# Differential scores: two of the three terms of a map stacked over 128 rows, the third as 64-row pairs

## The reference

```python
def differential_attention(q, k, v, lam):   # q,k: (B,H,2,T,Dh), H = 8, Dh = 64; v: (B,H,T,2Dh)
    def block(args):                         # 128 queries
        s = jnp.einsum('bhiqd,bhikd->bhiqk', qb, k) * scale     # i: the two maps
        s = s - (slopes[:, None, None] * dist[None])[None, :, None]
        p = jax.nn.softmax(s, axis=-1)
        a = p[:, :, 0] - lam * p[:, :, 1]
        return jnp.einsum('bhqk,bhkd->bhqd', a, v)
```

## Time and profile before

| | |
|---|---|
| median of 3 runs (lowest to highest) | 2536.93 us (2536.89 to 2537.68) |
| profiled execution | 2532.99 us, span 2531.0 us |
| mean granted TensorE clock | 0.997 |
| busy: TensorE, VectorE, ScalarE, GpSimd | 2502.5, 1758.6, 1155.8, 413.7 us |
| attention of layer 1 | from 1252 to about 1775 us |

### The profile page before, as it was taken

How to read it: one execution, slowest core, us unless ns; L and a number is a source line. 1 busy time by engine, 2 the same in 40 slices (tenths; PEclk the granted TensorE clock), 3 DMA queues, 4 the chain that set the end, 5 groups by cost and what they waited for, 6 DMA issues and landing times.

```text
span 2531.0 us, 34993 instructions
## 1 busy us (share of the span) xinstructions
PE 2502.5 (99%) x12931; PEld 2065.0 (82%) x12931; DVE 1758.6 (69%) x2647; ACT 1155.8 (46%) x2016; POOL 413.7 (16%) x320
## 2 busy tenths in 40 slices
PE   9999999899999999999999999999999999999998
PEld 7888777688888888888888888888888888888887
DVE  6556565656878878666577777777657878887654
ACT  6555554625333333444455455556343333334434
POOL 1001022400332333100000000000002333232001
PEclk9999999999999999999999999999999999999999
DMA  3222253633444444866211111111334444447764
GB/s 130 61 60 74 53 134 94 186 127 117 147 178 162 146 171 166 316 216 210 80 48 50 50 50 50 48 49 71 117 108 143 168 155 164 156 154 268 237 194 145
DMA packets 189171, 332.38 MB, mean 131 GB/s; under 512 B 59728, under 2 KB 67792, under 8 KB 180816
## 3 DMA queue, kind: packets, MB, share of 16 engines
q1 hardware_dynamic: 154208, 320.62, 37.5%
q10 hardware_dynamic: 34800, 9.60, 1.8%
HBM read 238.24 MB, written 91.91 MB: 130 GB/s over the span
## 4 chain that ended last, share of the span: by engine, by line
PE 93%; issue 2%; DVE 2%; ACT 1%; DMA 1%; SPq 1%; POOL 0%; ACTq 0%; POOLq 0%; DVEq 0%
PE PS L2381 20%; PE PS L2296 18%; PE PS L2297 18%; PE PS L2298 18%; PE PS L2545 4%; PE PS L2477 4%; PE PS L2501 3%; PE PS L2493 1%; PE PS L2448 1%; PE PS L2522 1%; PE PS L2395 1%; PE PS L2462 1%; PE PS L2304 1%; PE PS L2526 1%; PE PS L2438 0%
## 5 line engine op out<-in xcount | busy, mean ns | idle before, releaser
L2381 PE MATMUL PS<-HH,WS 128*128 128x512 f32 x1536 | 515.9, 402 | 3.5 <-DVE HL L1623 1.1
L2381 PEld LDWEIGHTS PS<-HH,WS 128*128 128x128 f32 x1536 | 285.5, 188 | 59.9 <-issue 1.6
L2381 PE MATMUL PS<-HL,WS 128*128 128x512 f32 x768 | 301.4, 393 | 0.0
L2097 DVE TENSOR_TENSOR SPLIT<-RAWI,SPLIT 128x1024 fp32r<-128x1024 f32 x154 | 194.2, 1265 | 149.9 <-ACT SPLIT L1450 149.9
L1450 ACT ACTIVATE SPLIT<-RAWI 128x1024 fp32r<-128x1024 f32 x154 | 162.9, 1060 | 205.7 <-PE PS L2298 152.2
L2296 PE MATMUL PS<-TH,WS 128*128 128x512 f32 x640 | 249.2, 389 | 2.3 <-ACT SIL L1442 2.3
L2298 PE MATMUL PS<-TH,WS 128*128 128x512 f32 x640 | 249.0, 389 | 0.0
L2297 PE MATMUL PS<-TL,WS 128*128 128x512 f32 x640 | 249.0, 389 | 0.0
L2296 PE MATMUL PS<-SPLIT 128*128 128x512 f32 x616 | 240.2, 390 | 0.0
L2298 PE MATMUL PS<-SPLIT 128*128 128x512 f32 x616 | 239.7, 389 | 0.0
L2297 PE MATMUL PS<-SPLIT 128*128 128x512 f32 x616 | 239.7, 389 | 0.0
(11 more groups left out here) (274 smaller groups left out, 4969.8 us busy)
## 6 DMA issues: line engine op xcount, KB each, us to landing
WR<-wstrips SPq DMA_DIRECT2D x224, 256.0 KB, 2.7
RAWI<-ab_scratch SPq DMA_DIRECT2D x154, 256.0 KB, 4.2
ab_scratch<-SIL SPq DMA_DIRECT2D x132, 256.0 KB, 2.0
WD<-wdown SPq DMA_DIRECT2D x22, 1024.0 KB, 7.5
wd_scratch<-WD SPq DMA_DIRECT2D x22, 1024.0 KB, 3.9
RAWI<-wd_scratch SPq DMA_DIRECT2D x88, 256.0 KB, 3.3
UR<-wstrips SPq DMA_DIRECT2D x80, 256.0 KB, 3.3
RAWI<-wdown SPq DMA_DIRECT2D x66, 256.0 KB, 3.8
```

The source lines that it names most:

```text
L2097: e.tensor_tensor(SPLIT[m % 6][:, 1], RAWI[:, m % 4], f(SPLIT[m % 6][:, 0]), ALU.subtract).then_inc(S["ilo"], 1)
L2381: last = e.matmul(ps, wt, xt, start=g == 0, stop=g == 23)
```

## The change

A tile QLOW is added. For layer 1 KS and QS are laid out by map: in slot m the rows of map m hold the high part, and the other 64 rows hold, for K, map m's low part, and for Q, map m's high part again. So one matmul over 128 rows gives high x high + high x low of a map. The third term, Q low x K high, has QLOW and stays in 64-row matmuls, two side by side.

To fill the other rows there is a new ScalarE function `kq_cross`: two copies of 64 x 512 from the staging slot across the halves. `kq_low` writes K's low part back into the staging slot and Q's into QLOW. `kq_high` and `kq_low` are two instructions of 64 rows each instead of one of 128. `kq_cross` for K waits for `kq_low`. It stands behind the exps of the step, and in `begin(1)` between the roundings. `qk` and some evacuations wait for a new semaphore `kq_crossed`; `pick_ready` is folded into `consts_ready`. In `begin(1)` 18 matmuls of chunk 0 go ahead of the first `qk` and 6 behind it.

```diff
@@ pool_program, kq_low(P, k)
+            if P >= 8:
+                for m in range(2):
+                    r = map_rows(m)
+                    high = KS[r, P % 2, m, c:c + 512] if k < 4 else QS[r, m, c:c + 512]
+                    low = staged(k, r) if k < 4 else QLOW[r, c:c + 512]
+                    last = e.tensor_tensor(low, staged(k, r), f(high), ALU.subtract)
+                last.then_inc(S["kq_lo"], 1)
+                return
@@ act_program, kq_high(P, k)
+            if P >= 8:
+                for m in range(2):
+                    r = map_rows(m)
+                    to = KS[r, P % 2, m, c:c + 512] if k < 4 else QS[r, m, c:c + 512]
+                    last = e.activation(to, staged(k, r), ACT.Copy)
+                last.then_inc(S["kq_hi"], 1)
+                return
             e.activation(high[:, c:c + 512], staged(k), ACT.Copy).then_inc(S["kq_hi"], 1)
+
+        def kq_cross(P, k):
+
+            c = 512 * (k % 2)
+            if k < 4:
+                e.wait_ge(S["kq_lo"], 4 * P + k - 1)
+            for m in range(2):
+                to = KS[map_rows(1 - m), P % 2, m, c:c + 512] if k < 4 else QS[map_rows(1 - m), m, c:c + 512]
+                last = e.activation(to, staged(k, map_rows(m)), ACT.Copy)
+            last.then_inc(S["kq_crossed"], 1)
@@ act_program, begin(layer)
-            for k in range(3, 5) if layer else range(2, 6):
-                kq_high(P0, k)
-            if layer == 0:
+            if layer:
+                kq_high(P0, 3)
+                kq_cross(P0, 2)
+                kq_cross(P0, 3)
+                kq_high(P0, 4)
+                kq_cross(P0, 4)
+            else:
+                for k in range(2, 6):
+                    kq_high(P0, k)
@@ act_program, attention_diff()
                     if after:
                         exp(*after, m, "C")
+                for v in rounded(P, n):
+                    kq_cross(*v)
                 if last:
@@ dve_program, evac(P, k, bank=None)
             if late(P):
+                if P >= 8 and k == 2 and P > 8:
+                    e.wait_ge(S["kq_crossed"], crossed_to(P - 1, 5))
+                elif P >= 8 and k in (5, 0, 1):
+                    e.wait_ge(S["kq_crossed"], crossed_to(P, {5: 2, 0: 3, 1: 4}[k]))
@@ pe_program, qk(P, n)
             e.wait_ge(S["kq_lo"], 4 * P + (3 if n < 4 else 4))
+            e.wait_ge(S["kq_crossed"], crossed_to(P, 4 if n < 4 else 5))
             e.wait_ge(S["exp_done"], 1 + 16 * P + 2 * n)
...
-            for c in range(0, nk, 4):
-                wd = 128 * min(4, nk - c)
-                k = slice(128 * (k0 + c), 128 * (k0 + c) + wd)
-                for i, (a, b) in enumerate(((0, 0), (0, 1), (1, 0))):
-                    for m in range(2):
-                        r = slice(64 * m, 64 * m + 64)
-                        last = e.matmul(PS[:, S_BANK[m] + c // 4, 0:wd], QS[r, a, q], KS[r, P % 2, b, k],
-                                        start=i == 0, stop=i == 2)
+            for h in range(2):
+                for m in range(2):
+                    e.matmul(PS[:, S_BANK[m] + h, :], QS[:, m, q], KS[:, P % 2, m, half(h)], start=True, stop=False)
+            for h in range(2):
+                for m in range(2):
+                    r = map_rows(m)
+                    last = e.matmul(PS[:, S_BANK[m] + h, :], QLOW[r, q], KS[r, P % 2, m, half(h)], start=False, stop=True)
@@ pe_program, begin(layer)
-            fill(P0, 0, 0, 14, layer, bank=PV_BANK)
+            fill(P0, 0, 0, 18, layer, bank=PV_BANK)
             qk(P0, 0)
-            fill(P0, 0, 14, 24, layer, bank=PV_BANK)
+            fill(P0, 0, 18, 24, layer, bank=PV_BANK)
```

More of the change, by code:

```diff
@@ L171, in build @@
     PICK = sb("PICK", [128, 64], f32r)
+    QLOW = sb("QLOW", [128, T], f32r)
     assert place[0] <= nc.sbuf_usable_end
@@ L275, in bias_tile, with staged, map_rows, crossed_to @@
         return BIASC[:, par, :] if kind == "C" else (BIAS1 if par else BIAS0)
-    def staged(k):
-        return FS[:, 512 * ((k % 3 + 1) % 3):512 * ((k % 3 + 1) % 3) + 512]
+    def staged(k, r=slice(0, 128)):
+        return FS[r, 512 * ((k % 3 + 1) % 3):512 * ((k % 3 + 1) % 3) + 512]
+    def map_rows(m):
+        return slice(64 * m, 64 * m + 64)
+    def crossed_to(P, k):
+        return 4 * (P - 8) + k - 1
     VFLAT = FS[:, 512:3 * 512 + BAND]
@@ L342, in build @@
                  "hsq_done hhi_done hlo_done hadd hsum_done hsqrt_done hrinv_done hspread_done hrstd_done "
-                 "fill_done fill_evac kq_hi kq_lo tv_done vhi_done vlo_done "
+                 "fill_done fill_evac kq_hi kq_lo kq_crossed tv_done vhi_done vlo_done "
                  "bias_full0 bias_full1 qk_done ttr_done exp_done rec_done "
@@ L347, in build @@
                  "rb_full4 rb_full5 rb_full6 rows_turned rows_copied rows_out rwide_done lspread_done ymul_done st_done st_copy ct_out cn_full cd_done ce_done cw_done al_half al_done a_out mgy_full mgz_full mga_full mg_done ym_out "
-                 "yhi_done ylo_done ysq_done yssq_done yeps_done ymean_done ysqrt_done yrec_done yspread_done ynorm_done rt_turned rt_high rt_low pick_ready op_half "
+                 "yhi_done ylo_done ysq_done yssq_done yeps_done ymean_done ysqrt_done yrec_done yspread_done ynorm_done rt_turned rt_high rt_low op_half "
                  "raw_full2 raw_full3 raw_full4 raw_full5 raw_full6 raw_full7 product_done s_ready copied c11_added c22_added c21_added "
@@ L1966, in attention_diff @@
                     flat = "p k t -> p (k t)"
-                    e.tensor_tensor(PICK[:, :], IDENT[:, 0:64], IDENT[:, 64:128], ALU.add).then_inc(S["pick_ready"], 1)
-                    e.memset(RT[:, KC - 1, :], 1.0).then_inc(S["pick_ready"], 1)
+                    e.tensor_tensor(PICK[:, :], IDENT[:, 0:64], IDENT[:, 64:128], ALU.add).then_inc(S["consts_ready"], 1)
+                    e.memset(RT[:, KC - 1, :], 1.0).then_inc(S["consts_ready"], 1)
                     e.scalar_tensor_tensor(out=EL[:, :, :].rearrange(flat), in0=L0[:, :, :].rearrange(flat),
@@ L2683, in attention_diff @@
             e.wait_ge(S["yrec_done"], 1)
-            e.wait_ge(S["pick_ready"], 2)
+            e.wait_ge(S["consts_ready"], 4 + 2)
             e.transpose(PS[0:64, FILL_BANK, 128:256], RT[:, :, :].rearrange("p k t -> p (k t)"),
```

## The result

| | before | after |
|---|---|---|
| median (lowest to highest) of 4 runs each | 2536.91 us (2536.52 to 2537.68) | 2553.61 us (2552.53 to 2560.76) |
| ratio after / before, 95% interval | | 1.0080 (1.0068 to 1.0092) |
| profiled execution, its span | 2532.99, 2531.0 us | 2553.2, 2551.4 us |
| busy: TensorE, VectorE, ScalarE, GpSimd | 2502.5, 1758.6, 1155.8, 413.7 us | 2507.8, 1761.8, 1218.9, 457.2 us |

The forecast was 2537.7 us (2535.6 to 2542.2) and no change. The kernel is 16.7 us slower, 11.4 us above the range.

The account below looks back on a forecast made before the run. TensorE was taken to bound the kernel, with 93% of the span. Blocks -1.0, start +1.2, pairs +0.2 and tail +0.4 gave +0.8 us: 2537.7 us, range 2535.6 to 2542.2, no change.

Parts of the forecast that it names:

- Together 1.91: Block of scores on TensorE: six slots as before, still 1.91 us; 0.015 us a block won, -1.0 us in all.
- Rival 4: Score blocks: the change of rows behind 128-row matmuls costs nothing, 12.8 us faster, 2525 us; chance 0.06.
- +1.2 us: Start of layer 1: the later first block and longer blocks on an idle array lose 1.2 us of TensorE time.
- I take 1.29: Start of layer 1: GpSimd's two 64-row halves overlap and take 1.29 us together; upper bound 2.55.
- Rival 1: Start of layer 1: GpSimd takes the halves one after the other, +3.2 us in all, 2540.1 us; chance 0.25.
- Two copies in a row take 1.16 us, each further one 0.53: ScalarE: price of 64-row copies, used for the rounding halves and crossings at the start and in the pairs.
- rival 2: Start of layer 1: on top of rival 1 the clock falls, 2541.8 to 2543.5 us, say 2542.5; chance 0.12.
- Theory C: Rival explanation set up for the follow-up runs, not in the forecast: the clock causes the loss; no size given.
- That holds by 0.1 to 0.2 us: Pairs: Q's crossings end in time for the fifth block and the next pair's first, with 0.1 to 0.2 us spare.
- +0.2: The other seven pairs: ScalarE's crossings cost 0.2 us in all, bounds 0 and +4.5.
- Rival 3: Pairs: crossings pass the two gates by 0.2 us at 15 places, +3 us, 2540.7 us; chance 0.12.
- 2 x 0.19 = +0.4: Tail: two blocks of the last pair start behind an exp on an idle array, each 0.19 us longer.

Follow-up runs that it names:

- e1_pairs: Changed kernel with each block of scores again as twelve 64-row matmuls, all roundings, subtractions and crossings as changed; 2554.27 us, ratio 1.0070.
- e4: Kernel before with layer 1's roundings and subtractions split into 64-row halves, no crossings, old matmuls; 2539.41 us, ratio 1.0017.
- e3: Changed kernel with Q's first half rounded ahead of K's crossings at the start of layer 1; 2550.81 us, ratio 1.0060.
- e7: e6 with the crossings at the start of layer 1 on VectorE too; 2539.34 us, ratio 1.0012.
- e8: e7 with the subtraction of Q's first half at the start of layer 1 on VectorE as well; 2538.35 us, ratio 1.0012.
- e2: Changed kernel with crossing copies cut from 512 to 8 columns from P = 10 on; 2544.08 us, ratio 1.0034.
- e10: e6 with the order of e3 at the start of layer 1; 2539.11 us, ratio 1.0008.
- e5: Changed kernel with K's crossings in the pairs moved on ScalarE behind the output copy and weight split; 2553.21 us, ratio 1.0060.
- e9: Pair 8 and the start of layer 1 as in the kernel before, pairs 9 to 15 as e6; 2533.83 us, ratio 0.9992.
- e6: e5 with Q's crossings in the pairs done by VectorE, those at the start of layer 1 still on ScalarE; 2542.07 us, ratio 1.0024.

## Why the prediction was wrong

**The block: right.** "Together 1.91", 0.015 us a block to be won: away from the gates it is 1.897 against 1.905, 0.008 a block, within the bounds. Rival 4 is out, since the 0.32 comes back inside the block. The Trainium skill ("TensorEngine Tiling (Array Packing)", Key Properties) has the array drain where the tiling mode changes, and this agrees. e1_pairs has the same result from the other side. So nothing was there to pay for the feeding.

**The start: "+1.2 us" was +7.0.** Four things made it: the halves on GpSimd, the copies on ScalarE, a term that I left out, and the clock.

**The halves on GpSimd: "I take 1.29".** They took 2.57 to 3.00 us. Rival 1, "GpSimd takes the halves one after the other", at 0.25, was right. The Trainium skill's "GPSIMD Engine Reference", section 2.1, on which I leaned, has each core begin the next instruction when its own share is done; the halves start 1.35 us apart, wherever they stand back to back. So they don't overlap here; why not, no run tells. With what VectorE loses beside them they are 2.4 of e4's 2.8 us at the first block. Of the 5.4 us by which that block is later in the changed kernel, this and the order (2.5, e3) are the two large parts.

**"Two copies in a row take 1.16 us, each further one 0.53".** 64-row copies take 0.63 and start 0.64 to 0.65 apart: ScalarE's 128-row weight splits next to them are still 1.15 a pair. From the rounding of K's second half to Q's stand four copies, each 0.11 dearer than I had it.

**A term that I left out.** VectorE's weight split stands beside GpSimd. Before, GpSimd's single subtraction ended 0.42 us into it, and the two splits took 1.58 us together. Beside two halves they take 1.24 and 1.78 us, so the evacuation of K's second half comes at 1249.43, and with it the rounding at 1250.14, counted from the same first matmul 1.7 us later than before. GpSimd's second half is longer too, 1.65 for 1.29. The Trainium skill's page "SBUF — State Buffer", section "Who interferes with whom", states the rule that I didn't look for: a VectorE instruction with two SBUF inputs contends with a GpSimd one that reads SBUF, for a shared port that is an exclusive lock, and the order of issue decides which of them waits. The rows agree: the first split ends at 1247.81, 0.56 behind GpSimd's first half (1247.25), and the second at 1249.51, 0.55 behind its second half (1248.96). The copies of e7 and e8 have only one SBUF input, so that sentence doesn't cover them; beside GpSimd they took over three times as long all the same.

Rival 1 had the first block near 1255.4. Counted from the same first matmul it started at 1257.56 (1259.42 less the 1.86 by which the two traces differ there), 2.2 us later still: 1.6 are the later rounding of K's second half, for which I had allowed 0.2, and 0.4 the four copies.

**The clock: rival 2, at 0.12, happened.** I had priced a fall at 1.7 to 3.4 us on top of a wait of 2.4. The wait was 4.8 us and the clock fell to 0.50 for 6.8 us. Theory C holds in part: e3, with 2.3 us and no fall, gives back 3.9 us for 2.5 of wait, so the fall cost 1.4. Its length didn't matter: in e2, with the same wait, it was 3.4 us, and the start cost 7.05. Only the way to the first block's bias-add was longer by it (3.38 us in both, 1.99 in e3); from there to the second block, which waits for the exps, it is 3.9 us in all three. All waits of 3.1 to 4.8 us at this place had a fall in them or just behind, those of 2.3 us (e3, e10) none. That doesn't make 2.3 us safe elsewhere: at the fifth block of the last pair, 2.4 us behind the matmul ahead of it in four traces, a fall of 3.4 us came within 1.2 us of the block's start in e1, e3 and e5, and none in the changed kernel.

**The pairs: "That holds by 0.1 to 0.2 us".** It didn't, by 0.5 us at seven fifth blocks and 0.8 at seven first ones: +10.3 us for the "+0.2", with bounds to +4.5 that were too narrow. I had the crossings' end 0.01 us behind the start of the last fill; it is 0.58 behind it (1425.28 - 1424.70). The rounding in halves starts the copy of the transposed weights 0.2 later; the exp's read ends 3.36 us behind that copy's start (1423.99 - 1420.63) instead of 3.22, 0.14 more; and the crossings end 1.29 us behind the read, not 1.07. The block starts 0.1 us behind their end. At the first block comes one more: "The output copy and the weight split behind it (1413.24) come 0.4 later, and so does VectorE's half of the split and with it the next bias-add". In the step ahead of the first block it is the evacuation of Q behind that split that matters, and with it Q's rounding and its crossing: 0.33 a pair (e5). Rival 3 named these places with 0.2 us each; the place was right, the size not.

**The tail: "2 x 0.19 = +0.4".** It was +1.2. I had the last pair's fifth block start behind an exp, and it starts behind Q's crossing, which ends 1.3 us behind the second exp's read (1763.99 - 1762.69): it comes 1.6 us later behind the matmul ahead of it than before. In front of the sixth block, 0.55 us of idle time are gone in return (0.65 before, 0.10 now).

The two large terms together make 17.3 us, near the medians' 16.7, and e9, without both, is back at the time of before.

## What to carry to other kernels

Where two half-array matmuls run side by side, putting two terms one above the other wins no TensorE time; count slots before paying for the layout. An instruction takes its time by its columns: two of 64 rows cost twice one of 128, on ScalarE and on GpSimd, so price a split at double, and look at what runs beside it on VectorE. On a chain that gates TensorE with 0.1 us to spare, put the new work on another engine, or behind what feeds the next gate (e6), even if the engine that gets it is the busier one.

## What the runs showed of the hardware that I had not expected

- GpSimd: two subtractions of 64x512 on rows 0 to 63 and 64 to 127 start 1.35 us apart and take 1.29 each, as one of 128x512 does.
- ScalarE: 64-row copies in a row start 0.64 us apart, 0.63 long; two of 128 rows take 1.15 together.
- VectorE beside GpSimd's subtractions: a 128x512 subtraction from SBUF 1.24 and 1.78 us instead of 0.68, a 64x512 copy 1.37 and 1.42 instead of 0.43.
- TensorE's clock: with waits of 3.1 to 4.8 us at the start of layer 1 it was 0.50 (1.2 GHz) for 3.4 or 6.8 us, with 2.3 us it stayed at 1.00; with 2.4 us at one block of the last pair it was 0.50 for 3.4 us in three traces and 1.00 in the changed kernel's. The fall at the start cost 1.4 us, in e2, where it lasted 3.4 us, as in the changed kernel with 6.8.
